# The residual input of the first row group: VectorE adds it, and GpSimd issues its loads

## The reference

```python
def _rmsnorm(x, g):
    xf = x.astype(jnp.float32)
    y = xf * lax.rsqrt(jnp.mean(xf * xf, axis=-1, keepdims=True) + RMS_EPS)
    return (y * g.astype(jnp.float32)).astype(x.dtype)
...
    out = jnp.concatenate([attn, y_ssm], axis=-1) @ w_out     # (rows, 2048) @ (2048, 2048)
    y = x + gate * _rmsnorm(out, g_post)
    return y, (k, v, ik, h_last.real.astype(x.dtype), h_last.imag.astype(x.dtype))
```

## Time and profile before

| what | value |
|---|---|
| times of three runs | 2353.95, 2356.22, 2356.24 us; median 2356.22 |
| profiled execution | 2358.88 us, span of its records 2357.1 us |
| TensorE matmuls | 2134.6 us busy, 91% of the span |
| VectorE, ScalarE, GpSimd | 1238.4, 719.7 and 432.4 us busy |
| mean granted clock of TensorE | 0.945 |
| first chunk of the second group | 2119 to 2190 us |

### The profile page before, as it was taken

How to read it: one execution, slowest core, us unless ns; L and a number is a source line. 1 busy time by engine, 2 the same in 40 slices (tenths; PEclk the granted TensorE clock), 3 DMA queues, 4 the chain that set the end, 5 groups by cost and what they waited for, 6 DMA issues and landing times. The chain is left out here.

```text
span 2357.1 us, 33442 instructions
## 1 busy us (share of the span) xinstructions
PE 2134.6 (91%) x12705; PEld 1887.5 (80%) x12705; DVE 1238.4 (53%) x2433; ACT 719.7 (31%) x1406; POOL 432.4 (18%) x703
## 2 busy tenths in 40 slices
PE   6898898999999999999999994878995899998896
PEld 4578887888999999999999993767783578776774
DVE  6455564544335888878776653565553251223124
ACT  5331122111133333333332213444441243221321
POOL 0253442555300000000000002342331200004001
PEclk8999999999999999999999996999997599999997
DMA  9963366555443333334343316533203232227336
GB/s 346 335 159 92 110 142 159 159 178 169 126 109 90 90 93 94 94 85 107 94 101 96 81 48 196 149 99 93 65 19 78 67 79 76 72 74 219 100 94 178
DMA packets 357898, 283.66 MB, mean 120 GB/s; under 512 B 107833, under 2 KB 299521, under 8 KB 356457
## 3 DMA queue, kind: packets, MB, share of 16 engines
q1 hardware_dynamic: 332050, 244.63, 38.0%
q10 hardware_dynamic: 24368, 33.18, 4.2%
q0 software_dynamic: 1328, 3.80, 0.5%
HBM read 221.34 MB, written 60.20 MB: 119 GB/s over the span
## 5 line engine op out<-in xcount | busy, mean ns | idle before, releaser
L1281 PE MATMUL ps_z<-h_hi,w_hi 128*128 128x384 f32 (+2 forms) x1936 | 666.3, 344 | 0.0
L1283 PE MATMUL ps_z<-h_hi,w_lo 128*128 128x384 f32 (+2 forms) x1936 | 656.9, 339 | 0.0
L1282 PE MATMUL ps_z<-h_lo,w_hi 128*128 128x384 f32 (+2 forms) x1936 | 656.7, 339 | 0.0
L1281 PEld LDWEIGHTS ps_z<-h_hi,w_hi 128*128 128x128 f32 (+1 forms) x1936 | 363.1, 188 | 15.7 <-issue 5.4
L1282 PEld LDWEIGHTS ps_z<-h_lo,w_hi 128*128 128x128 f32 (+1 forms) x1936 | 363.2, 188 | 5.1
L1283 PEld LDWEIGHTS ps_z<-h_hi,w_lo 128*128 128x128 f32 (+1 forms) x1936 | 362.7, 187 | 5.4
L865 DVE TENSOR_TENSOR w_lo<-w_raw,w_hi 128x512 fp32r<-128x512 f32 (+1 forms) x172 | 123.4, 718 | 352.6 <-ACT w_hi L531 351.1
L2624 DVE TENSOR_TENSOR o_lo<-o_raw,o_hi 128x512 fp32r<-128x512 f32 x128 | 89.2, 697 | 282.4 <-ACT o_hi L2580 282.2
L531 ACT ACTIVATE w_hi<-w_raw 128x512 fp32r<-128x512 f32 (+1 forms) x172 | 107.5, 627 | 260.2 <-DMA w_raw<-in_w_in 202.6
L2580 ACT ACTIVATE o_hi<-o_raw 128x512 fp32r<-128x512 f32 x128 | 81.1, 634 | 310.9 <-PE ps_out L2765 247.2
L997 DVE MAX8 top<-score 128x8 f32<-128x1024 f32 (+5 forms) x192 | 171.1, 891 | 3.4
(11 more groups left out here) (435 smaller groups left out, 3273.3 us busy)
## 6 DMA issues: line engine op xcount, KB each, us to landing
w_raw<-in_w_in SPq DMA_DIRECT2D x176, 256.0 KB, 3.1
wada<-in_w_ada SPq DMA_DIRECT2D x32, 1024.0 KB, 9.5
o_raw<-in_w_out SPq DMA_DIRECT2D x128, 256.0 KB
wg<-in_w_ada SPq DMA_DIRECT2D x32, 512.0 KB, 5.0
zt<-z_sb ACTq DMA_DIRECT2D x28, 576.0 KB, 4.3
g_raw<-in_w_glu SPq DMA_DIRECT2D x24, 512.0 KB, 4.2
xs<-in_x_prompt SPq DMA_DIRECT2D x8, 1024.0 KB, 8.1
iq_raw<-zt SPq DMA_DIRECT2D x48, 128.0 KB, 3.3
```

The source lines that it names most:

```text
L1281: M(to, w_hi[q][:, k, 0:m], h_hi[:, kk, cols], start=kk == 0, stop=False)
L1282: M(to, w_hi[q][:, k, 0:m], h_lo[:, kk, cols], start=False, stop=False)
L1283: return M(to, w_lo[q][:, k, 0:m], h_hi[:, kk, cols], start=False, stop=kk == KB - 1)
```

## The change

VectorE adds x for the first group, in its own order, right after `o_lo` of the step two after the gates and ahead of the next half's scaling. The loads of x go from SyncE's queue to GpSimd's. GpSimd runs through all twenty finals: it waits until VectorE has added the final two before, and issues the final's transfers. It adds nothing in that chunk any more. Loads for finals 0 and 1 have nothing to wait for. The second group's finals are as before.

```diff
             def send(g, c, kb):
-                for f in finals_at(g, c, kb - 2):
-                    if f >= 2:
-                        sp.wait_ge(y_ok[f % 2], f // 2)
-                    load_x(sp, 0, f)
                 for H in half_at(g, c, kb - 4):
                     store_half(sp, 0, H)
...
-            for g in range(2):
-                for f, (i, q) in enumerate(finals[g]):
-                    n = before[g] + f
-                    if g and n % 2:
-                        continue
-                    part = rows[i][:, OC * q:OC * q + OC]
-                    k, slot, x = x_piece(g, f)
-                    pool.wait_ge(x_in[g][slot], x_landed(g, k))
-                    pool.wait_ge(scaled, n + 1)
-                    nc.gpsimd.tensor_tensor(part, part, x, ALU.add).then_inc(y_ok[n % 2], 1)
+            for f in range(len(finals[0])):
+                if f >= 2:
+                    pool.wait_ge(y_ok[f % 2], f // 2)
+                load_x(pool, 0, f)
+            for f, (i, q) in enumerate(finals[1]):
+                n = before[1] + f
+                if n % 2:
+                    continue
+                part = rows[i][:, OC * q:OC * q + OC]
+                k, slot, x = x_piece(1, f)
+                pool.wait_ge(x_in[1][slot], x_landed(1, k))
+                pool.wait_ge(scaled, n + 1)
+                nc.gpsimd.tensor_tensor(part, part, x, ALU.add).then_inc(y_ok[n % 2], 1)
...
+            def add_x(g, f):
+                i, q = finals[g][f]
+                n = before[g] + f
+                part = rows[i][:, OC * q:OC * q + OC]
+                k, slot, x = x_piece(g, f)
+                dve.wait_ge(scaled, n + 1)
+                dve.wait_ge(x_in[g][slot], x_landed(g, k))
+                V.tensor_tensor(part, part, x, ALU.add).then_inc(y_ok[n % 2], 1)
...
+                    for f in finals_at(g, c, kb - 2):
+                        add_x(0, f)
                     for f in finals_at(g, c, kb - 1):
                         scale(0, f)
+                for f in finals_at(g, c, KB - 2):
+                    add_x(0, f)
```

More of the change, by code:

```diff
@@ L2713, in _ @@
                 scale(1, f)
[L2714 to L2720, removed]
+                if (before[1] + f) % 2:
+                    add_x(1, f)
         @block.tensor
```

## The result

The change makes the kernel slower, by 0.4%:

| | median us | runs | ratio to before, 95% interval |
|---|---|---|---|
| before | 2354.74 | 2353.72 to 2356.24, 6 | |
| after | 2364.19 | 2362.43 to 2367.42, 6 | 1.0041 [1.0028, 1.0054] |

What follows compares the result with a forecast made beforehand. TensorE's matmuls, busy 91% of the span, were taken to bound the kernel. Removing 11.3 us, adding 2.9 of waits for x and 1.9 for scattered landings gave -6.5, a median of 2349.7 us; range 2344.5 to 2358.5.

Steps and rivals of the forecast that it cites:

- The chunk's account: Second row group's first chunk, before: 71.1 us, with 49.9 of work, 11.3 lost inside and 7.35 waiting at its end.
- I take the removal at its full 11.3 us: Inside the chunk: taking x loads and their wait off SyncE recovers all 11.3 us of gaps and low clock.
- 20 adds of 0.69 us in the hole: On VectorE: adds fit the 1.6 us between `o_lo` and the scaling; uncovered they would cost 14 us.
- The issue at 0.55 us: On GpSimd: each x transfer takes 0.55 us to issue, bounds 0.51 and 0.75.
- rival 3: VectorE's two-input instructions hold up GpSimd's queue: slower by 5 to 6 us, 2362 us; chance 0.12.
- I take 3.3 to 3.5, bounds 2.9 and 4.4: On GpSimd's queue: assumed us from the start of an x piece's last transfer to its data.
- L: In the x loads: time from the last transfer's start to its data, forecast at 3.3 to 3.5 us.
- rival 2: The wait only changes its engine: 8.8 us lost at L = 4.0, some 12 at 4.4; chance 0.31.
- The loop: Each of two x slots cycles through issue, L and add, 5.1 us; lateness totals 2.4 us at L = 3.3.
- None of the gaps is as long as the shortest behind which the clock fell (2.58): On TensorE: new gaps stay under 2.58 us, so no slow step is added.
- The chunk's end stays: Next chunk's first matmul still waits 7.35 to 7.6 us, its weights issued behind the last store.
- The signs: Expected profile: VectorE waits about 12 us for x, TensorE's gaps at steps 9 and 12, chunk 63 to 66 us.

Runs made afterwards that it cites:

- f: The changed kernel with eight x slots instead of two and the first group's last two stores issued by GpSimd: 2335.88 us, ratio 0.9922 to before.
- d_slots8: The changed kernel with eight x slots instead of two: 2343.57 us, ratio 0.9937 to before.
- a: The kernel before with only the adds moved to VectorE, SyncE still issuing the x loads: 2352.31 us, ratio 0.9987 to before.
- c: The changed kernel without the stores of the first group's output rows, waits for the adds kept: 2344.99 us, ratio 0.9953 to before.
- j: The changed kernel with eight x slots, the last two first-group stores issued by GpSimd, and x loads issued by SyncE: 2339.6 us, ratio 0.9921 to before.
- d_slots4: The changed kernel with four x slots instead of two: 2346.36 us, ratio 0.996 to before.
- e: The changed kernel with the x loads issued by ScalarE, behind its `o_hi`, instead of GpSimd: 2357.86 us, ratio 1.0008 to before.
- b_pool_both: The kernel before with only the x loads moved to GpSimd, which still makes the adds: 2368.77 us, ratio 1.0046 to before.
- k: The kernel before with the first group's last two stores issued by GpSimd behind its adds: 2352.24 us, ratio 0.9985 to before.
- i_store_later: The changed kernel with each of SyncE's first-group stores one step later: 2355.87 us, ratio 1.0006 to before.

## Why the prediction was wrong

**The chunk's account (49.9 of work, 11.3 lost inside, 7.35 at the end): right.** f comes down to 52.2 us.

**"I take the removal at its full 11.3 us": right only where x is in time.** In d_slots8 the gaps inside are 0.77 and 0.28. In after itself VectorE never waited for `o_hi` inside the chunk, so the old loss was gone there too, and the new wait took its place. The step said that the store left on SyncE "asks for adds that lie right behind an `o_lo` that SyncE has seen already". In after those adds stood up to 4.80 us behind that `o_lo`, and SyncE waited 41.6 us for them. Inside the chunk this was no second loss: the weights behind the store need the next `o_lo`, and VectorE makes that only behind the same adds. It was right to charge the wait once, on VectorE.

**20 adds of 0.69 us in the hole: right.** 0.681 to 0.695 us each; a shows that they cost nothing.

**The issue at 0.55 us: right**, 0.48 to 0.55, also beside VectorE's two-input instructions (the transfer of 2165.04 lies beside the `o_lo` of 2164.99). So rival 3 had the right side and nearly the time (2362), but by luck: its mechanism didn't occur. The Trainium skill (SBUF — State Buffer, "SBUF: two separate sides") words its trap so that such instructions hold up only a GpSimd instruction that reads SBUF; the trace agrees, by these issues. The other half of it was in the rows already, though the prediction said that none shows it: an `o_lo` beside GpSimd's add, which reads SBUF, took 1.43 us instead of 0.69.

**"I take 3.3 to 3.5, bounds 2.9 and 4.4": this is the step that failed.** L was 5.2 us in the mean. The rows it came from were SyncE's x loads, which stood ahead of the store in the same queue, and GpSimd's loads in a stretch at a DMA share of 0.19. Neither had a store released at the same moment in another queue. c measured 3.3 with the stores' transfers gone, so these make 1.9 us of it. As rival 2 I had priced the same mechanism at 8.8 us for L = 4.0 and 12 for 4.4, that is 8 per us of L; carried on to 5.2 it gives 18, and 17.3 were measured. -11.3 + 17.3 = +6.0, and the chunk grew by 7.0. The loop was worked out rightly: at c's L of 3.3 it gave 2.4 us and 2.7 were measured. It was given the wrong L, and the bounds of L ended too early.

The page of the Trainium skill that the prediction cited (DMA: Bandwidth & Descriptors, "Issuing engines are not separate DMA queues") says that the queues share the same 16 engines. I read out of that only that L gains nothing. The same page ("Queues, rings and completion order") has each of these engines take turns, packet by packet, between the queues that hold work for it. By that rule x in a queue of its own shares with the store where it had been ahead of it, which is a loss. The trace agrees as to the loss: 256 KB of x landed after 3.3 us in SyncE's queue (four loads) and 4.6 in GpSimd's (two), with the DMA engines at 0.68 and 0.61. From after:

```profile
q1 hardware_dynamic: 3824, 9.18, 39.8%
q0 software_dynamic: 2144, 4.72, 21.4%
...
x_add<-in_x_prompt POOLq DMA_DIRECT2D x4, 192.0 KB, 4.3
...
x_add<-in_x_prompt POOLq DMA_DIRECT2D x2, 256.0 KB, 4.6
x_add<-in_x_sample POOLq DMA_DIRECT2D x16, 32.0 KB, 3.2
```

x is the whole of the queue in the second row, weights and stores that of the first. That the sharing is packet by packet is the page's statement; the runs show only that the store's company costs 1.9 us, and that its moment counts.

**"None of the gaps is as long as the shortest behind which the clock fell (2.58)": wrong twice.** The gaps were longer (3.35 and 3.29), and the one of 2.13 us was also followed by slow matmuls, from 1.5 us into its step. The length of the gap alone doesn't decide: slow matmuls also came behind gaps of 1.46 us (in j) and 1.50 (in d_slots4), and none behind one of 2.48 (in e). So nothing in the two rows it was read from made 2.58 a bound.

**The chunk's end stays: right**, 6.84 us.

**The signs.** VectorE waited 30.4 us for x where 12 were expected, most of it on the second x of a pair, as said. TensorE's gaps stood at steps 5, 6, 8, 12, 13 and 15, expected at 9 and 12. The chunk took 78.1 us, expected 63 to 66.

## What to carry to other kernels

Before moving a load to another queue, ask what the event that releases it releases besides: in one queue the load you need soonest can stand first, in two it shares with the rest, and its landing is not that of either queue alone. A landing time costs only through the number of buffers, so where a load is bound to an engine's instruction by a two-buffer loop, add buffers first (here worth 0.3% in the kernel before and, from 1.0041 to 0.9937, 1.0% after the change), and then see who should issue. And when a queue stands in front of an engine's result, ask what it would wait for next. If that lies behind the same result in the engine's own order, the wait costs nothing more (the 41.6 us of SyncE in after). If it doesn't, what stands behind it in the queue comes late (the 55.5 us in b_pool_both, and SyncE's wait in front of the last stores, worth about 3.8 us in k).

## What the runs showed of the hardware that was not expected

- A transfer of 256 KB took 3.3 us to land in SyncE's queue ahead of a store (median of four), 4.6 us in GpSimd's beside it, 4.9 in ScalarE's beside it, and 3.0 in GpSimd's without the store (two each), while the DMA engines were busy for 0.50 to 0.68 of the time. Single loads of x took up to 6.5 us at 0.61.
- GpSimd issues such a transfer in 0.48 to 0.55 us, whatever its size from 32 to 256 KB and whatever VectorE does meanwhile.
- TensorE's matmuls took 0.63 us instead of 0.40 in a part of the step behind gaps of 1.46 us (j_sp_slots8_end), 1.50 (d_slots4), 1.84 (i_store_later) and 2.13 (after); behind gaps of 1.63 (i_store_later), 1.72 (c_no_stores) and 2.48 us (e_act_queue) they did not.
